# Operand buffers at chosen distances modulo 256 bytes, small rows behind the large buffers

## The reference

```python
def first_block(x, mem, ...):
    h = rmsnorm(x, g_mix)
    proj = h @ w_in                      # queries, keys, values of three attentions, three gates
    o_swa = sliding_window_attention(...)
    o_dsa = dsa_attention(...)           # the best 64 keys of an index score
    o_mem = memory_cross_attention(...)
    merged = g0 * (o_swa @ w_proj_swa) + g1 * (o_dsa @ w_proj_dsa) + g2 * (o_mem @ w_proj_mem)
    x = x + merged @ w_out
    hid = square(relu(rmsnorm(x, g_mlp) @ w_mlp_in))
    return rmsnorm(x + hid @ w_mlp_out, g_final)

def second_block(x, ...):
    for layer in range(2):
        if layer == 1: shared = nsa_shared_kv(h, ...)
        h = post_norm(h, 0.5 * swiglu(h, w1, w3, w2))        # 1024 -> 2816 -> 1024
        mix = chunked_sgu_mixer(h) if layer == 0 else nsa_mixer(h, shared)
        h = post_norm(h, mix)
        h = post_norm(h, 0.5 * swiglu(h, w1, w3, w2))
```

## Time and profile before

| | |
|---|---|
| median of 3 runs | 1536.14 us (1534.89 to 1536.82) |
| the profiled execution | 1536.11 us, span of its instructions 1534.3 us |
| granted TensorE clock, mean | 0.985 of full speed |
| TensorE matmul busy | 1486.0 us, 97% |
| VectorE, ScalarE, GpSimd busy | 931.1, 659.4 and 95.6 us |
| read from HBM | 261.92 MB |

### The profile page before, as it was taken

How to read it: one execution, slowest core, us unless ns; L and a number is a source line. 1 busy time by engine, 2 the same in 40 slices (tenths; PEclk the granted TensorE clock), 3 DMA queues, 4 the chain that set the end, 5 groups by cost and what they waited for, 6 DMA issues and landing times.

```text
span 1534.3 us, 25330 instructions
## 1 busy us (share of the span) xinstructions
PE 1486.0 (97%) x10484; PEld 1359.3 (89%) x10484; DVE 931.1 (61%) x1363; ACT 659.4 (43%) x834; POOL 95.6 (6%) x78
## 2 busy tenths in 40 slices
PE   8989999999999999998999999999999998999997
PEld 6978987898999999998889999999999886799996
DVE  5886367555666555657775555646545757655556
ACT  5665533333434334444153334425333457543332
POOL 0012141000020000100020000100000100100000
PEclk9999998999999999999999999999999999999999
DMA  7443435776677555565355555666555430465551
GB/s 252 147 135 110 148 120 173 208 221 202 199 247 239 179 179 202 182 192 180 117 200 167 191 186 180 203 192 227 192 187 174 158 120 26 137 215 177 184 191 56
DMA packets 191526, 268.43 MB, mean 175 GB/s; under 512 B 5740, under 2 KB 164752, under 8 KB 191182
## 3 DMA queue, kind: packets, MB, share of 16 engines
q1 hardware_dynamic: 186336, 250.05, 49.8%
q0 software_dynamic: 4224, 15.91, 3.0%
q10 hardware_dynamic: 878, 1.21, 0.3%
HBM read 261.92 MB, written 4.19 MB: 173 GB/s over the span
## 4 chain that ended last, share of the span: by engine, by line
PE 85%; DVE 9%; ACT 3%; issue 1%; DMA 1%; POOL 0%; SPq 0%; DVEq 0%; ACTq 0%
PE bank L739 84%; PE bank L762 2%; DVE split L1998 2%; ACT split L1528 1%; DVE resid L2075 1%; DVE resid L2083 1%; DVE stats L2054 1%; DVE resid L2052 1%; DMA ring<-in_ffn_w 1%; DMA ring<-in_w_in 1%; ACT act_out L1550 0%; DVE arena L2590 0%; DVE msq L2061 0%; DVE arena L2195 0%; ACT gain_rows L1654 0%
## 5 line engine op out<-in xcount | busy, mean ns | idle before, releaser
L739 PE MATMUL bank<-hT_hi,split 128*128 128x256 f32 (+1 forms) x3984 | 736.0, 284 | 7.2 <-ACT act_out L1666 5.4
L1998 DVE TENSOR_TENSOR split<-ring,split 128x2048 fp32r<-128x2048 f32 x212 | 484.2, 2285 | 387.2 <-ACT split L1528 381.9
L739 PEld LDWEIGHTS bank<-hT_hi,split 128*128 128x128 f32 (+1 forms) x3984 | 620.4, 189 | 15.1 <-issue 9.5
L1528 ACT ACTIVATE split<-ring 128x2048 fp32r<-128x2048 f32 (+1 forms) x224 | 426.8, 1906 | 368.0 <-PE bank L739 334.2
L739 PE MATMUL bank<-hT_lo,split 128*128 128x256 f32 (+1 forms) x1992 | 561.6, 282 | 0.0
L739 PEld LDWEIGHTS bank<-hT_lo,split 128*128 128x128 f32 (+1 forms) x1992 | 378.1, 190 | 2.2
L739 PE MATMUL bank<-split,hid_hi 128*128 128x512 f32 x992 | 290.4, 399 | 0.0
L739 PEld LDWEIGHTS bank<-split,hid_hi 128*128 128x128 f32 x992 | 183.9, 189 | 40.6 <-issue 0.8
L739 PE MATMUL bank<-split,hT_hi 128*128 128x256 f32 (+1 forms) x896 | 178.6, 297 | 6.3 <-DVE split L1998 4.4
L739 PE MATMUL bank<-split,hid_lo 128*128 128x512 f32 x496 | 160.1, 396 | 0.0
L739 PEld LDWEIGHTS bank<-split,hT_hi 128*128 128x128 f32 x896 | 143.4, 190 | 14.7 <-DVE split L1998 5.0
(11 more groups left out here) (216 smaller groups left out, 973.5 us busy)
## 6 DMA issues: line engine op xcount, KB each, us to landing
ring<-in_ffn_w SPq DMA_DIRECT2D x132, 1024.0 KB, 5.1
ring<-in_w_in SPq DMA_DIRECT2D x19, 1024.0 KB, 5.1
ring<-in_w_mlp_in SPq DMA_DIRECT2D x16, 1024.0 KB, 6.3
ring<-in_w_mlp_out SPq DMA_DIRECT2D x16, 1024.0 KB, 5.0
ring<-in_sgu_w_in SPq DMA_DIRECT2D x16, 1024.0 KB, 5.4
ring<-in_sgu_w_out SPq DMA_DIRECT2D x8, 1024.0 KB, 4.9
ring<-in_kv_w SPq DMA_DIRECT2D x6, 1024.0 KB, 5.2
ring<-in_w_out SPq DMA_DIRECT2D x4, 1024.0 KB, 4.9
```

The costliest lines, as they stand in the source:

```text
L739: ins = pe.matmul(o, lhsT, rhs, start=start, stop=stop)
L1528: act.activation(halves(q, n)[0], ring[:, u % SLOTS, 0:n], ACT.Copy).then_inc(hi_ready, 1)
L1998: dve.tensor_tensor(lo, ring[:, u % SLOTS, 0:n], hi.bitcast(F32), ALU.subtract).then_inc(split_ready, 1)
```

## The change

Nothing is computed otherwise, and the instructions of every engine stand in the same order with the same waits, row for row. What changes is where buffers lie. A new helper `place(offset)` inserts an unused gap, so that the next buffer begins at the given offset modulo 256 bytes. It is called ahead of `ring`, `hid`, `arena`, `split` and `const`. `arena` and `split` are declared ahead of the small rows now, which so move behind the large buffers. `arena` is 24 words longer; its last used word is number 14471, as before.

```diff
-ARENA = 14472
+ARENA = 14496
+LINE = 256
...
+        def place(offset):
+
+            base = -(-nc.sbuf_base // 32) * 32
+            gap = (offset - base) % LINE
+            if gap:
+                sb(f"gap{base}", [P, gap // 4])
+
...
+        place(128)
         ring = sb("ring", [P, SLOTS, UNIT])
...
+        place(64)
         with nc.sbuf_tensor("shared_rows", [P, 3 * MLP_BODY * 512], F32) as shared_rows:
             pass
         hid = sb("hid", [P, MLP_BODY, 512])
         hid_hi = sb("hid_hi", [P, MLP_BODY, 2, S], F32R)
         hid_lo = sb("hid_lo", [P, MLP_BODY, 2, S], F32R)
         hid_tok = hid[:, 2, :].rearrange("p (b c) -> p b c", b=NB)
+        place(128)
+        with nc.sbuf_tensor("arena", [P, ARENA], F32) as arena:
+            pass
+        two = sb("two", [P, 2, KT, S], F32R)
+        sb("arena_rest", [P, ARENA - 2 * KT * S])
+        place(192)
+        split = sb("split", [P, SPLIT, 2, UNIT], F32R)
+        place(128)
         const = sb("const", [P, N_CONST])
...
-        with nc.sbuf_tensor("arena", [P, ARENA], F32) as arena:
-            pass
-        two = sb("two", [P, 2, KT, S], F32R)
-        sb("arena_rest", [P, ARENA - 2 * KT * S])
...
-        split = sb("split", [P, SPLIT, 2, UNIT], F32R)
```

## The result

The changed kernel takes 1497.85 us (median of 4 runs, 1496.87 to 1499.89) where the kernel before takes 1535.76.

A forecast was written before the change was run, and what follows sets the result against it. The prediction took TensorE's matmul spacing to bound the kernel. Gains of 10.4 us (`hT` on `split`) and 3.0 us (`split` on `hid`), other terms nothing, summed to -13.4 us: 1536.1 to 1522.7 us, range 1503 to 1539.

The forecast's parts named there:

- The bound: Whole kernel: TensorE is busy 1486.0 of 1534.3 us, so what matters is how closely matmuls follow each other.
- the first term of the sum: `hT` on `split`, distance 96 to 192: spacing 119.9 to 118.0 ns, 5496 matmuls counted, 10.4 us gained.
- the slower rival: `hT` on `split` falls into a dear rhythm at 192: 121.4 ns gives 1541.3 us, worst 125 ns gives 1561; chance 0.18.
- The bound below: Best case for `hT` on `split` at 192: 116.7 ns, the cheapest row's spacing, 17.6 us gained.
- all of the loss goes: Matmuls on line 739 reach 108.5 ns (256 columns) and 215.7 ns (512): 100.7 us gained, 1435.4 us; chance 0.05.
- Waited away: Of 912 `hT` on `split` matmuls before 300 us and between 1210 and 1335 us, half count; TensorE waits there.
- Split on hid: 512-column matmuls, distance 160 to 128: 2.0 ns less spacing for each of 1488, 3.0 us gained.
- Split on hT, and VectorE: 1200 matmuls at distance 160 to 64: 0.4 us, put at nothing; VectorE's split operations stay within 20 ns of 2292.
- The small rows: Rows moved behind the large buffers keep their place modulo 256, so their few accesses cost what they did: nothing.
- The four probability places: In the last attention, four places before and after, so that half of the title changes nothing.
- Distance costs nothing: Spacing differences belong to the kind of matmul, not its place: no change, 1536.1 us; chance 0.12.
- More than the neighbours show: Multiples of 64 do better: 116.7 ns for both 256-column kinds, 22.2 us gained, 1513.9 us; chance 0.25.

The follow-up runs named there:

- the kernel before with one gap: Kernel before with only a 160-byte gap ahead of `split`, so it starts at 192 modulo 256: 1494.58 us timed, ratio 0.9751.
- split at 32: Changed kernel with `split` alone put back to 32 modulo 256, so `hT` on `split` at distance 96 again: 1533.25 us.
- The low-half experiment: Changed kernel with only the low half of each place of `split` moved 96 bytes further, to distance 96 from `hT`: 1519.60 us.

## Why the prediction was wrong

**The bound was read rightly.** What the change gained lies in the spacing of the matmuls on line 739. Some 5900 spacings by 119.9 - 113.7 = 6.2 ns are 36.6 us of the 42.5 by which TensorE's busy time fell; the 512 columns give 1488 x 1.3 = 1.9 us, and the rest is of the size of what the clock gave back (3.6 us above), for which the sum had no term.

**The step that failed is the first term of the sum: the spacing at distance 192.** I took 118.0 ns from the neighbours 160 and 224. The neighbours themselves were right, though read on other pairs of buffers: for `hT` on `split` they measure 118.5 and 118.3. The failure was to read the value between them off these two. The spacing is no smooth function of the distance; 192 is a notch of 5 ns between them. The term was 1.9 ns and is 6.2. I had written as much under the slower rival (not smoothly by distance) and had used it in one direction only.

**The bound below was too narrow for the same reason.** It took the cheapest mean of any row, 116.7 ns, and the low end of the whole range some 115; measured are 113.7. Nothing in the trace excluded a distance that none of its rows shows from doing better than all of them. The range should have run further towards "all of the loss goes", of which over half came true for this pair: 6.2 of 11.4 ns.

**Waited away.** I let half of the 912 matmuls outside the dense stages pass. In the first stage even less came through: 576 matmuls of `hT` on `split` lie ahead of `two` on `split` there, worth at most 3.6 us, and it begins at 187.78 us where it began at 188.69. The long dense stage, on the other hand, passed nearly everything on: TensorE's idle time in it was 7.4 us before (300 to 1210 us) and is 8.2 now (293 to 1180). The sum of both is 39.2 us of span against 42.5 us of busy time.

**Split on hid.** Forecast 2.0 ns from the row of `two` on `hid` at distance 128; 1.3 measured. The direction was right, and 1488 x 1.3 = 1.9 us instead of 3.0.

**Split on hT, and VectorE.** Both as said: 117.4 ns on average against 117.6 before, and 2293 ns against 2292.

**The small rows** changed nothing, as forecast: the kernel before with one gap is as fast. The four probability places are the same in both kernels, so no run tests them.

**The rivals.** "Distance costs nothing" fell with split at 32. So falls, for this kernel, the rule of the Trainium skill, page "SBUF — State Buffer", section "Who interferes with whom", that TensorE's two reads are independent. The low-half experiment shows one of its reads paying 9 ns for the place of the other. The slower rival did not come true at 192, where the dear rhythm (117.8 ns) is still cheaper than the 119.9 before; but a dear rhythm at that distance exists, and most tiles took it behind 512 columns at distance 0. "More than the neighbours show" had the right direction and the wrong reason: 0 and 128 are multiples of 64 too and read 119.9 and 119.0.

## What to carry to other kernels

Where TensorE is the bound and each matmul brings its own weights, measure the spacing of matmuls from start to start for each pair of buffers, and compare it with rows that have none of the loss (here 215.7 ns for 512 columns of bf16 zeros, and 109 for a transpose of 128 columns of fp32, the nearest row to 256 columns). If it is several ns above, sweep the distance between the moving and the stationary buffer modulo 256 bytes with one gap, over all eight multiples of 32: a value between two measured ones can't be interpolated. Time the whole more than once, since the cheapest distance of one pair (0 for 512 columns here) can leave the next pair in its dear rhythm.

## What the runs showed of the hardware

- The spacing of 256-column fp32r matmuls, each with its own weight load, depends on the start distance of moving and stationary operand modulo 256 bytes. For `hT` on `split` it is 113.7 ns at 192, 117.2 to 117.3 at 64, 118.3 at 224, 118.5 at 160, 119.0 at 128, 119.9 at 0 and 96; at 32 `split` on `hT` read 117.0. Moving all buffers by 32 bytes changed nothing (113.7 ns).
- The partner in the collision is the load of the next matmul's weights (123.2 ns against 114.3).
- At distances 64 and 192 two steady rhythms exist, 113.4 and 117.8 ns, and one lasts through up to 16 tiles, 384 matmuls. The same program can take either in two executions.
- Work of the other engines and of the DMA engines does not change these numbers: 113.4 ns both with DMA engines 60% busy and with none, and with VectorE busy 34.08 of 40 us and 5.63 of 10.70.
- At the lower clock (granted 0.5) the loss is not seen: 213 to 214 ns from start to start at distance 96 before and at 192 after.
